# Wide matmuls over high and low inputs in the output projection and the second feed-forward product of a two-block fp32 model

## What is computed

```
y  = gated sum over branches           # [tokens, 1024]
x  = x + y @ w_out                     # output projection, "wo"
h  = rmsnorm(x)
g  = f(h @ w_in)                       # first feed-forward product, "ff", 2 x 2816 wide
x  = x + g @ w_ffn_down                # second feed-forward product, "down", 2816 -> 1024
```

## Time and profile of the kernel before

| | |
|---|---|
| median of 3 executions | 2410.05 us (2409.16 to 2410.96) |
| profiled execution, span | 2408.8 us |
| TensorE, matmuls | 2324.3 us busy (96%), 19438 matmuls |
| TensorE, weight loads | 2236.5 us (93%), 19438 loads |
| VectorE | 1822.3 us (76%) |
| ScalarE | 1336.1 us (55%) |
| GpSimd | 381.4 us (16%) |
| DMA | 366.67 MB, mean 152 GB/s |
| mean granted TensorE clock | 0.993 |

### The profile page before, as it was taken

One profiled execution on the slowest core, in us unless ns is written; L12 is line 12 of the kernel. 1 busy time (PEld: TensorE's weight loads), 2 busy tenths in 40 slices (PEclk: granted clock), 3 DMA queues, 4 the chain that ended last, 5 costly groups with the idle time before them and its releaser, 6 DMA issues.

```text
span 2408.8 us, 51528 instructions
## 1 busy us (share of the span) xinstructions
PE 2324.3 (96%) x19438; PEld 2236.5 (93%) x19438; DVE 1822.3 (76%) x3501; ACT 1336.1 (55%) x2308; POOL 381.4 (16%) x484
## 2 busy tenths in 40 slices
PE   6999999999999999999999998999999999999998
PEld 6998999899999999899899997988999998899998
DVE  5689856788876588966788885788886668888764
ACT  5655556756555655556666554655554465556443
POOL 0000002626930000002635940000000000000000
PEclk9999999999999999999999998999999999999999
DMA  5433343344555433343344553443555544445553
GB/s 212 158 124 121 108 149 115 123 150 165 174 174 172 166 137 114 116 145 129 117 149 167 181 179 123 167 140 125 174 183 182 186 161 147 132 149 179 183 184 130
DMA packets 100437, 366.67 MB, mean 152 GB/s; under 512 B 11632, under 2 KB 12144, under 8 KB 99824
## 3 DMA queue, kind: packets, MB, share of 16 engines
q1 hardware_dynamic: 100208, 363.53, 45.1%
HBM read 362.44 MB, written 1.05 MB: 151 GB/s over the span
## 4 chain that ended last, share of the span: by engine, by line
PE 57%; DVE 26%; DVEq 6%; ACT 5%; issue 4%; ACTq 1%; DMA 1%; SPq 0%
PE psum L460 56%; DVE ring_lo L1397 7%; ACT arena L925 2%; DVE arena L1447 2%; DVE arena_r L1385 1%; DVE arena L1439 1%; ACT ring_hi L938 1%; DVE arena_r L1383 1%; DVEq L1873 1%; DVEq L1377 1%; DVE arena L1621 1%; DVEq L1900 1%; DVE arena L1618 1%; DVE arena L1455 1%; ACT hn_hi L925 1%
## 5 line engine op out<-in xcount | busy, mean ns | idle before, releaser
L460 PE MATMUL psum<-hn_hi,ring_hi 128*128 128x272 f32 (+2 forms) x3792 | 1114.8, 294 | 35.9 <-DVE ring_lo L1397 21.9
L460 PE MATMUL psum<-hn_hi,ring_lo 128*128 128x272 f32 (+2 forms) x3792 | 1087.3, 287 | 0.0
L460 PE MATMUL psum<-hn_lo,ring_hi 128*128 128x272 f32 (+2 forms) x3792 | 1078.6, 286 | 0.0
L1397 DVE TENSOR_TENSOR ring_lo<-ring,ring_hi 128x1024 fp32r<-128x1024 f32 x564 | 689.5, 1232 | 185.6 <-ACT ring_hi L938 148.3
L938 ACT ACTIVATE ring_hi<-ring 128x1024 fp32r<-128x1024 f32 x684 | 714.1, 1055 | 194.3 <-DMA ring<-w 164.4
L460 PEld LDWEIGHTS psum<-hn_hi,ring_hi 128*128 128x128 f32 x3792 | 724.6, 191 | 63.4 <-issue 37.9
L460 PEld LDWEIGHTS psum<-hn_hi,ring_lo 128*128 128x128 f32 x3792 | 725.0, 191 | 0.0
L460 PEld LDWEIGHTS psum<-hn_lo,ring_hi 128*128 128x128 f32 x3792 | 719.6, 191 | 1.6
L460 PE MATMUL psum<-arena_r,ring_hi 128*128 128x256 f32 (+2 forms) x3284 | 605.6, 285 | 5.5 <-DVE ring_lo L1397 3.0
L925 ACT ACTIVATE arena<-psum 128x272 f32<-128x272 f32 (+8 forms) x736 | 257.0, 366 | 582.0 <-PE psum L460 502.6
L2118 POOL TENSOR_TENSOR ring_lo<-ring,ring_hi 128x256 fp32r<-128x256 f32 x480 | 381.2, 829 | 1030.5 <-ACT ring_hi L938 1030.0
(11 more groups left out here) (158 smaller groups left out, 1455.0 us busy)
## 6 DMA issues: line engine op xcount, KB each, us to landing
ring<-w SPq DMA_DIRECT2D x684, 512.0 KB, 3.3
cst<-consts SPq DMA_DIRECT2D x1, 1960.0 KB, 14.2
x_sb<-x_meta SPq DMA_DIRECT2D x1, 1088.0 KB, 4.8
out<-x_sb SPq DMA_DIRECT2D x1, 1024.0 KB, 3.9
arena<-lam SPq DMA_DIRECT2D x1, 256.0 KB, 4.1
par_sb<-par SPq DMA_DIRECT2D x1, 193.0 KB, 4.7
pos_sb<-positions SPq DMA_DIRECT2D x1, 128.0 KB, 6.3
cst<-consts SPq DMA_DIRECT2D x1, 65.5 KB, 4.8
```

The source lines that it names most:

```text
L460: i = nc.tensor.matmul(out_, lhsT=lhsT, rhs=rhs, start=first, stop=last)
L1397: V.tensor_tensor(ring_lo[:, slot], ring[:, slot], ring_hi[:, slot].bitcast(F32), ALU.subtract)\
```

## The change

In five stages (`down` of block one's last layer, `wo` and `down` of both layers of block two) the products use a new helper, `wide_product`: the high and the low part of the input are read as one right-hand side of 2 x 256 columns (two runs at a fixed distance), against the high weights, into all 512 columns of the bank; then the low weights by the high input go into columns 0 to 255. So a weight block takes two matmuls, one of 512 and one of 256 columns, in place of three of 256. From the second block on the 256-column matmul comes first. The bank's two halves are then added to x by two dependent adds in place of one, and only after the second is the bank released and x signalled. The feed-forward up product, the other projections, the merges and block one's other stages keep `product`; the other edits (`hn` as one tensor at the same place, tuples with a third member) only make the views.

```diff
-        hn_hi = sb("hn_hi", KT * T1, F32R)
-        hn_sq = twin("hn_sq", KT * T1, F32)
-        hn_lo = sb("hn_lo", KT * T1, F32R)
-        hn_t = twin("hn_t", KT * T1, F32)
+        hn = sb("hn", 2 * KT * T1, F32R)
+        hn_f = twin("hn_f", 2 * KT * T1, F32)
...
+        def both_halves(at, apart, n):
+
+            return arena_r[:, at:at + 2 * apart].rearrange("p (s n) -> p s n", s=2)[:, :, 0:n]
...
+            def wide_product(b, key, rhs, ready=None, first=0):
+
+                ps = b.take(pe, key)
+                for i, (hi, _, both) in enumerate(rhs):
+                    w_hi, w_lo = weight_block()
+                    if ready is not None:
+                        pe.wait_ge(*ready[i])
+                    final = i == len(rhs) - 1
+                    if i == 0:
+                        mm(ps[:, :], w_hi, both[:, :, first:first + T2], True, False)
+                    mm(ps[:, 0:T2], w_lo, hi[:, first:first + T2], False, False)
+                    if i > 0:
+                        mm(ps[:, :], w_hi, both[:, :, first:first + T2], False, final, b.filled(key) if final else None)
+                    through()
+                b.ended(key, stream["n"])
...
-                    product(b1, ("down", j), [(FF[0][:, k, :], FF[1][:, k, :]) for k in range(FT)], T1,
-                            ready=[s1["ff"].upto(k) for k in range(FT)] if j == 0 else None, first=t0(True))
+                    ready = [s1["ff"].upto(k) for k in range(FT)] if j == 0 else None
+                    if layer < DEPTH - 1:
+                        product(b1, ("down", j), tiles_of(FF, FT, T1), T1, ready=ready)
+                    else:
+                        wide_product(b1, ("down", j), tiles_of(FF, FT, T1), ready, N_META)
...
-                    product(b2, ("wo", j), [(Y2S[0][:, k, :], Y2S[1][:, k, :]) for k in range(KT)], T2,
+                    wide_product(b2, ("wo", j), tiles_of(Y2S, KT),
                             ready=[s2["yb"].upto(k) for k in range(KT)] if j == 0 else None)
...
-                    product(b2, ("down", j), [(FF2[0][:, k, :], FF2[1][:, k, :]) for k in range(FT)], T2,
+                    wide_product(b2, ("down", j), tiles_of(FF2, FT),
                             ready=[s2["ff"].upto(k) for k in range(FT)] if j == 0 else None)
...
-                V.tensor_tensor(X[:, j, first:], X[:, j, first:], b.of(key)[:, first:tokens], ALU.add).then_inc(*b.free(key))
+                if now["stage"] == "two" or first == N_META:
+                    V.tensor_tensor(X[:, j, first:], X[:, j, first:], b.of(key)[:, T2:2 * T2], ALU.add)
+                    V.drain()
+                    V.tensor_tensor(X[:, j, first:], X[:, j, first:], b.of(key)[:, 0:T2], ALU.add).then_inc(*b.free(key))
+                else:
+                    V.tensor_tensor(X[:, j, first:], X[:, j, first:], b.of(key)[:, first:tokens], ALU.add).then_inc(*b.free(key))
                 fence(s["x"].done(key))
```

More of the change, by code:

```diff
@@ L275, in program @@
         X1 = x_sb[:, :].rearrange("p (k t) -> p k t", t=T1)
-        H1, L1, Q1, N1 = [t[:, :].rearrange("p (k t) -> p k t", t=T1) for t in (hn_hi, hn_lo, hn_sq, hn_t)]
-        H2, L2, Q2, N2 = [t[:, 0:KT * T2].rearrange("p (k t) -> p k t", t=T2) for t in (hn_hi, hn_lo, hn_sq, hn_t)]
+        H1, L1, Q1, N1 = [t[:, half * KT * T1:(half + 1) * KT * T1].rearrange("p (k t) -> p k t", t=T1)
+                          for t in (hn, hn_f) for half in range(2)]
+        H2, L2, Q2, N2 = [t[:, half * KT * T1:half * KT * T1 + KT * T2].rearrange("p (k t) -> p k t", t=T2)
+                          for t in (hn, hn_f) for half in range(2)]
+        HL2 = hn[:, :].rearrange("p (s n) -> p s n", s=2)[:, :, 0:KT * T2]
         OUT2 = x_sb[:, 0:KT * T2].rearrange("p (k t) -> p k t", t=T2)
@@ L486, in product @@
                 ps = b.take(pe, key)
-                for i, (hi, lo) in enumerate(rhs):
+                for i, (hi, lo, *_) in enumerate(rhs):
                     w_hi, w_lo = weight_block()
@@ L582, in _, with tiles_of @@
             hn1 = [(H1[:, k, :], L1[:, k, :]) for k in range(KT)]
-            hn2 = [(H2[:, k, :], L2[:, k, :]) for k in range(KT)]
+            hn2 = [(H2[:, k, :], L2[:, k, :], HL2[:, :, k * T2:(k + 1) * T2]) for k in range(KT)]
+            xg1 = [(XG1[0][:, k, :], XG1[1][:, k, :]) for k in range(KT)]
+            def tiles_of(split, n, width=T2):
+                return [(split[0][:, k, :], split[1][:, k, :], split[2][:, :, k * width:(k + 1) * width]) for k in range(n)]
             def projection(key):
@@ L645, in _ @@
                     products_across_norm(
-                        b1, tiles[:AHEAD], XG1, T1, [s1["xgh"].upto(("next", k), layer - 1) for k in range(KT)],
+                        b1, tiles[:AHEAD], xg1, T1, [s1["xgh"].upto(("next", k), layer - 1) for k in range(KT)],
                         [s1["xgl"].upto(("next", k), layer - 1) for k in range(KT)],
@@ L726, in _ @@
                 products_across_norm(
-                    b1, up[:AHEAD], XG1, T1, [s1["xgh"].upto(("ffn", k)) for k in range(KT)],
+                    b1, up[:AHEAD], xg1, T1, [s1["xgh"].upto(("ffn", k)) for k in range(KT)],
                     [s1["xgl"].upto(("ffn", k)) for k in range(KT)],
@@ L770, in merge2 @@
                              2: [s2["os"].upto(("s", p)) for p in range(2)], 3: [s2["normed"].upto(p) for p in range(2)]}[n]
-                product(b2, ("mB", n, j), [(hi[:, k, :], lo[:, k, :]) for k in range(2)], T2, ready=ready)
+                product(b2, ("mB", n, j), tiles_of({0: OMS, 1: OCS, 2: OSS, 3: GGS}[n], 2), T2, ready=ready)
             def attention_scores(kind, h):
@@ L818, in _ @@
                     products_across_norm(
-                        b2, tiles[:AHEAD], XG2, T2, [s2["xgh"].upto(("next", k), layer - 1) for k in range(KT)],
+                        b2, tiles[:AHEAD], tiles_of(XG2, KT), T2, [s2["xgh"].upto(("next", k), layer - 1) for k in range(KT)],
                         [s2["xgl"].upto(("next", k), layer - 1) for k in range(KT)],
@@ L844, in _ @@
                 for h in range(MLA_HEADS):
-                    product(b2, ("qu", h), [(CQS[0][:, k, :], CQS[1][:, k, :]) for k in range(2)], T2)
+                    product(b2, ("qu", h), tiles_of(CQS, 2), T2)
                 pe.wait_ge(*s2["ckn"].upto())
@@ L906, in _ @@
                 products_across_norm(
-                    b2, up[:AHEAD], XG2, T2, [s2["xgh"].upto(("ffn", k)) for k in range(KT)],
+                    b2, up[:AHEAD], tiles_of(XG2, KT), T2, [s2["xgh"].upto(("ffn", k)) for k in range(KT)],
                     [s2["xgl"].upto(("ffn", k)) for k in range(KT)],
```

29 lines of the change are left out of this document (14 added, 15 removed).

## The result

The changed kernel takes 2415.91 us (median of 12 executions, 2414.81 to 2417.42), the kernel before 2410.94 us (12 executions, 2408.73 to 2411.69). The medians differ by 5.0 us. The ratio on record is 1.0023 [1.0015, 1.0031], which is 5.5 us, with an interval of 3.6 to 7.5: slower, by more than the executions scatter. The forecast was 2409.6 us and "within 0.2%"; the time lies in the range, at the figure of the slow rival (2415.9). The profiled execution has a span of 2414.2 us and took 2415.99 us.

The account below looks back on a forecast made before the run. TensorE, busy 96% of the span, was taken as the bound, with VectorE deciding behind `wo`. Terms -6.28 + 4.78 + 1.04 = -0.46 us on a 2408.8 span gave 2408.3, carried to a median of 2409.6 us; range 2400 to 2417.

Parts of the forecast that it names:

- slow rival: Every wide matmul: surcharge goes with columns or each run of 256, so nothing is saved; 2415.9 us; chance 0.20.
- Matmuls: Three pairs of load and matmul become two, saving 11.9 ns per block: 6.28 us in down, 0.76 per `wo` stage.
- The formula: Time difference is 5.82 us less 528 times the saving per block; slower by over 0.2% needs under 1.9 ns.
- row at half clock: Behind the change of blocks, starts 214 ns apart, 256 columns at 1.2 GHz without surcharge; cited for the slow rival.
- Second add in `wo`: VectorE's turn grows to 3.13 us, x comes 2.39 us late, TensorE waits 2.8 us; two stages cost +4.78 us.
- VectorE's lateness is absorbed: Rival: VectorE's turns in `wo` have more slack or a spare slab, so both stages gain; 2403.3 us; chance 0.12.
- Starvation, queues, weight DMAs: Low slabs in `wo` run three ahead and don't suffer; removed TensorE queue entries and unchanged weight DMAs cost nothing.
- Tails: Last add of each block's last `down` is uncovered before squares, sum and norm: +0.52 us twice, 1.04.
- The first `down` of block two: Second add hidden behind ScalarE's table load, taken at 0; without that cover 0.52 us.
- Clock: Half-clock stretches may shorten, lengthen or follow a `wo` wait: 0 in the sum, 1.6 us either way in the range.
- a wide matmul hides more: Rival: 512 columns hide the next weight load, no surcharge left, 18.9 us go in `down`; 2397.0 us; chance 0.10.

Follow-up runs that it names:

- `wo` alone: Wide matmuls and second adds only in block two's two output projection stages, all down stages as in the kernel before: 2415.34 us against 2411.55, ratio 1.0015.
- GpSimd's help: Changed kernel with GpSimd instead of VectorE making four low slabs per layer during block two's output projection: 2411.88 us against 2411.20 for the kernel before, ratio 1.0003.
- the widths: Probe of the kernel before, products two to eight of the last down given matmuls of 128 to 512 columns, output not the model's: one execution, 2428.95 us.

## Why the prediction was wrong

- **Matmuls: wrong, and the step that failed.** "I take 11.9 because 256 and 272 columns carry the same surcharge." It measured 1.6 to 2.2 ns per block, 1.06 us over the 528 blocks (176 x 1.6 + 352 x 2.2) instead of 6.28. The arm of 16 columns was too short: with 0.4535 ns per column and 2.2 per matmul, which fit 256 and 512, 272 columns take 125.6 ns, with 0.417 per column and 11.9 per matmul 125.2; measured were 125.4. The rival was dismissed with the extreme of no constant at all (126.2), while what was measured lies between that and a full constant. The formula, 5.82 us less 528 times the saving, gives 4.8 us slower with some 2 ns, close to the 5.0 and 5.5 measured. That is partly luck: of its 5.82, `wo` was 0.8 too high and the tails 0.3 too low, and the clock was left out (below). Of the row at half clock, "so a pair need not cost it" was the right hint and was given too little weight.
- **Second add in `wo`: right in mechanism and place, somewhat oversized.** The turn took 3.08 us (forecast 3.13), the second add 0.49 (0.52), the lateness 2.1 (2.39), the wait on block 6 of the first product across the norm 2.0 (2.8, of which 0.76 was the saving that did not come), the two stages together 4.0 us (4.78). "VectorE's lateness is absorbed" fell: `wo` alone costs 3.8 us, GpSimd's help returns it.
- **Starvation, queues, weight DMAs: right.** Nothing appeared there.
- **Tails: right in place, one undersized.** The add itself costs 0.50 us at each end (forecast 0.52; 1.71 and 1.69 us of wait ahead of the sums of squares where it was 1.21 and 1.20), but block one's tail grew by 0.86, so together it is 1.36 us and not 1.04. The first `down` of block two costs nothing, as forecast: 54.32 us over its seven products after the first (54.68 before), and TensorE waits for nothing in the 10 us behind it.
- **Clock: right that it could come.** The sum by rows, -1.06 + 4.0 + 1.36 = 4.3 us, leaves 0.7 to the 5.0 of the medians and 1.2 to the 5.5 of the ratio. Three half-clock stretches behind eight waits, at 1.0 to 1.1 us, would be 0.8 us per execution by estimate. That this fills the gap is argued, not shown. The half-clock stretch behind block one also differs between executions: it ends at about 1498.8 us in the profile of the kernel before and at about 1500.8 in that of the changed kernel, though TensorE restarts earlier there.

So the slow rival was right in result and in its mechanism, "the surcharge goes with columns", which had been given one chance in five. The mechanism of "a wide matmul hides more" fell with the widths.

## What to carry to other kernels

Before merging matmuls, find the price per column and per instruction over a long arm (256 against 512 columns, in the operand type that the kernel uses): a surcharge over N/2.4 is not by that an overhead per instruction. A second dependent operation on an engine that is 84% busy in its stage is nearly free up to its slack (0.24 us per turn here) and then delays everything that waits on its last result; moving other work off that engine gave back what the matmuls could not. If such matmuls are the bound, try where their input tiles start: a shift of 16 elements made this kernel 6 us faster, where the change made it 5 us slower.

## What the runs showed of the hardware

- fp32r matmuls cost 118.3, 173.5 and 233.3 ns at 256, 384 and 512 columns, bf16 ones 108.2 and 216.1 at 256 and 512. At half clock the fp32r matmul of 256 columns took 214 ns, with no surcharge.
- fp32r matmuls of 128 and of 192 columns, each with its own weight load, cost the same, 111 ns; in bf16, 128 columns with their load cost 55. The Trainium skill ("TensorE: Matmul & The Clock Gate", LDWEIGHTS) puts a weight load at about P/1.2, 107 ns for 128 columns: close to what was seen for fp32r, but half as fast as the bf16 stream went, which loaded one tile throughout. That the load is what sets the 111 ns was not tried.
- The start of the input tile moves the pace of fp32r matmuls of 256 columns by 2 to 4 ns (116.7 to 120.8 in the arena, 117.9 to 120.0 in the normalised input), and the pace of one kind of product on one address went from 117.8 to 113.3 ns at a wait of 0.44 us within one execution and stayed there for 100 us.
- Of eight waits of 1.7 to 2.1 us in four executions, three were followed by a stretch at the lower of TensorE's two levels (some 3.4 us in the one that was timed), worth 1.0 to 1.1 us in the distance to the next `down`; behind the other five the clock stayed full.
